# 52 groups of nine products behind the last real product of a two-block transformer kernel

## The reference, cut to what matters

```python
def sq_relu_mlp(h, w_in, w_out):
    return jnp.square(jax.nn.relu(h @ w_in)) @ w_out
...
    m_lat = sq_relu_mlp(modulate(rms_norm(x, g_mlp_pre[i]), sh2, sc2), w_mlp_in[i], w_mlp_out[i])
    x = x + gt2 * rms_norm(m_lat, g_mlp_post[i])
...
return x
```

## Time and profile before

| | |
|---|---|
| median of 2 runs | 3484.51 us |
| the runs | 3483.55 and 3485.47 us |
| span of the profiled execution | 3485.0 us |
| PE busy | 3435.7 us (99%), 18494 records |
| DVE, ACT, POOL busy | 2166.1 (62%), 1318.3 (38%), 297.0 us (9%) |
| mean granted clock of PE | 0.996 |
| DMA | 452.01 MB, mean 130 GB/s |

### The profile page before, as it was taken

One profiled execution on the slowest core, in us unless ns is written; L12 is line 12 of the kernel. 1 busy time (PEld: TensorE's weight loads), 2 busy tenths in 40 slices (PEclk: granted clock), 3 DMA queues, 4 the chain that ended last, 5 costly groups with the idle time before them and its releaser, 6 DMA issues.

```text
span 3485.0 us, 46915 instructions
## 1 busy us (share of the span) xinstructions
PE 3435.7 (99%) x18494; PEld 2869.0 (82%) x18494; DVE 2166.1 (62%) x3570; ACT 1318.3 (38%) x1951; POOL 297.0 (9%) x376
## 2 busy tenths in 40 slices
PE   9999999999999999999999999999999999999998
PEld 7888967898888988895789888899988898588888
DVE  7555565656555655566676777788776557655444
ACT  4222453333222422246333523355523236643222
POOL 0000232001000100023100000012100001210000
PEclk9999999999999999999999999999999999999999
DMA  7544302434444344330243444345444311013221
GB/s 277 187 157 160 109 24 100 157 133 169 155 160 150 137 165 156 146 108 10 102 163 138 148 160 157 145 147 180 173 171 163 112 70 67 25 50 119 89 95 49
DMA packets 85562, 452.01 MB, mean 130 GB/s; under 512 B 10305, under 2 KB 12545, under 8 KB 48609
## 3 DMA queue, kind: packets, MB, share of 16 engines
q1 hardware_dynamic: 83168, 439.10, 34.2%
q0 software_dynamic: 2176, 9.92, 0.8%
HBM read 446.88 MB, written 2.10 MB: 129 GB/s over the span
## 4 chain that ended last, share of the span: by engine, by line
PE 89%; DVE 5%; ACT 3%; issue 1%; DMA 0%; POOL 0%; DVEq 0%; SPq 0%; ACTq 0%; POOLq 0%
PE ps L660 22%; PE ps L658 22%; PE ps L659 22%; PE ps L2774 2%; PE ps L2775 2%; PE ps L2776 2%; PE ps L3473 1%; PE ps L1035 1%; PE ps L1037 1%; ACT P L1855 1%; PE ps L1036 1%; PE ps L1772 1%; PE ps L1295 1%; PE ps L1297 1%; PE ps L1296 1%
## 5 line engine op out<-in xcount | busy, mean ns | idle before, releaser
L660 PE MATMUL ps<-nH,WL 128*128 128x512 f32 x2256 | 884.9, 392 | 0.0
L658 PE MATMUL ps<-nH,WH 128*128 128x512 f32 x2256 | 884.3, 392 | 0.4 <-ACT rot L3203 0.4
L659 PE MATMUL ps<-nL,WH 128*128 128x512 f32 x2256 | 883.1, 391 | 0.0
L564 DVE TENSOR_TENSOR WL<-raw,WH 128x2048 fp32r<-128x2048 f32 (+2 forms) x297 | 651.0, 2196 | 372.3 <-ACT WH L553 371.2
L553 ACT ACTIVATE WH<-raw 128x2048 fp32r<-128x2048 f32 (+2 forms) x299 | 543.3, 1822 | 574.4 <-PE ps L660 496.9
L658 PEld LDWEIGHTS ps<-nH,WH 128*128 128x128 f32 x2256 | 423.8, 188 | 95.2 <-issue 3.3
L659 PEld LDWEIGHTS ps<-nL,WH 128*128 128x128 f32 x2256 | 423.8, 188 | 93.7 <-issue 0.2
L660 PEld LDWEIGHTS ps<-nH,WL 128*128 128x128 f32 x2256 | 423.8, 188 | 91.5
L624 DVE SCALAR_TENSOR_TENSOR araw<-araw,cB 128x1024 f32<-128x1024 f32 x224 | 275.4, 1229 | 208.2 <-DMA araw<-in_ast 207.9
L658 PE MATMUL ps<-hH,WH 128*128 128x512 f32 x944 | 372.2, 394 | 1.0 <-DVE h L1262 1.0
L660 PE MATMUL ps<-hH,WL 128*128 128x512 f32 x944 | 371.3, 393 | 0.0
(11 more groups left out here) (452 smaller groups left out, 5919.6 us busy)
## 6 DMA issues: line engine op xcount, KB each, us to landing
raw<-in_wst SPq DMA_DIRECT2D x273, 1024.0 KB, 4.8
araw<-in_ast SPq DMA_DIRECT2D x225, 512.0 KB, 5.7
raw<-in_wst SPq DMA_DIRECT2D x18, 512.0 KB, 3.3
araw<-in_wst SPq DMA_DIRECT2D x9, 1024.0 KB, 4.8
row<-in_ast SPq DMA_DIRECT2D x15, 512.0 KB, 10.5
cw<-in_cw POOLq DMA_DIRECT2D x4, 1024.0 KB, 6.0
h<-in_xT SPq DMA_DIRECT2D x4, 512.0 KB, 5.5
raw<-in_wst SPq DMA_DIRECT2D x8, 256.0 KB, 2.7
```

Source lines behind the costliest of these rows:

```text
L564: dve.q.tensor_tensor(M.WL[k % NW][:, 0:n], M.raw[raw_use[k]][:, 0:n], M.WH[k % NW][:, 0:n].bitcast(F32), ALU.subtract).then_inc(*v_wlo.up(k))
L658: pe.q.matmul(to, hi[:, i, cc], xh, start=i == 0, stop=False)
L659: pe.q.matmul(to, hi[:, i, cc], xl, start=False, stop=False)
L660: t = pe.q.matmul(to, lo[:, i, cc], xh, start=False, stop=i == nk - 1)
```

## The change

A function `end_pe` is added, and PE's program calls it last. It takes the next two banks, `aside` for products of `ones` and `to` for the groups. It issues 20 pairs of products of `ones`, then 52 groups with such a pair behind each, and one product of `ones` at the end, which counts up a semaphore that nobody waits for. A group is nine products: three blocks of weights of slot 0 with the three terms each. Their moving operand begins at column 512 (i // 3) plus a shift. 16 groups are 512 columns wide with shifts from 48 to 108 in steps of 4 columns (16 bytes); 32 are 256 wide with shifts from 16 to 140 in steps of 4; four are 512 wide with the shift 48, and begin 0, 16, 32 and 48 columns further in the weights. What `nH`, `nL` and the slot hold then is what the kernel left there. The results are read by nobody.

```diff
+        def end_pe(pe):
+
+            nh, nl = (x[:, :, :].rearrange("p a b -> p (a b)") for x in (lat.nH, lat.nL))
+            two = [take("end", x) for x in range(2)]
+            for b, free in two:
+                pe.wait_ge(*free)
+            to, aside = two[0][0], two[1][0]
+
+            def between():
+                for _ in range(2):
+                    pe.q.matmul(aside[:, 0:128], M.ones[:, :], M.ones[:, :], start=True, stop=True)
+
+            def group(N, n, shift, at=0):
+                for i in range(n):
+                    w, x = ((0, 0), (0, 1), (1, 0))[i % 3]
+                    c = 512 * (i // 3) + shift
+                    pe.q.matmul(to[:, 0:N], (M.WL[0] if w else M.WH[0])[:, 128 * (i // 3) + at:128 * (i // 3) + 128 + at],
+                                (nl if x else nh)[:, c:c + N], start=i == 0, stop=i == n - 1)
+                between()
+
+            for _ in range(20):
+                between()
+            for x in range(16):
+                group(512, 9, 48 + 4 * x)
+            for x in range(32):
+                group(256, 9, 16 + 4 * x)
+            for x in range(4):
+                group(512, 9, 48, 16 * x)
+            t = pe.q.matmul(aside[:, 0:128], M.ones[:, :], M.ones[:, :], start=True, stop=True)
+            t.then_inc(*mm.up("end", 1))
+
...
             rest_pe(pe, attention2_pe(pe))
+            end_pe(pe)
```

## The result

The changed kernel took 3592.79 us (3590.22 and 3595.36) against 3484.51 before: a ratio of 1.0305, with a 95% interval of 1.0284 to 1.0325. It is slower by 3%, as forecast; the time is 6.8 us above the forecast of 3586. It lies inside the range of 3579 to 3597, but above the 3582 to 3590 to which the forecast gave 0.80.

The account below looks back on a forecast made before the run. PE, 99% busy, bounds the kernel. Tail start 3476.8 us plus clock 1.5, ones 32.4, groups 41.6 and 34.0, last record 0.2 and meeting 0.2 gave span 3586.7; less 0.5, 3586 us, range 3579 to 3597.

Parts of the forecast that it names:

- What bounds the kernel, and the cover: PE, busy for 99% of the span, bounds the kernel; its work ends 8.1 us before the end, hiding that much tail.
- Steps, not durations: In the groups, a product costs the distance between starts; pricing by durations would add 151 us, twice too much.
- The price of the places: In the groups, 0.231 us per 512-wide and 0.118 per 256-wide product: 41.6 and 34.0 us, nothing for shifted weights.
- Products of ones: In the tail, 145 products of two records each at 0.1117 us a record: 32.4 us.
- The clock: The tail begins in a trough at half clock, costing 1.5 us (1.0 to 3.0), with no further fall expected.
- The start and the banks: The tail starts at 3476.8 us, behind the root's spread, without waiting for its two banks, freed earlier by VectorE.
- From the span to the time: At the sum's end, 0.5 us off the 3586.7 span, since the span before was 3485.0 and the median 3484.5.
- Dearer places: Rival in the groups: shifted places cost longer steps, 3622 us in all or 3595 for a quarter of groups; chance 0.10.
- Cheaper places: Rival in the groups: shifted places cost shorter steps, 70.9 us for the groups and 3581 in all; chance 0.07.
- Clock, bank and end: Tail rivals: clock stays at half, 3692; bank freed late, 3592; end isn't PE's, time stays 3484.5; chance 0.01 each.

Follow-up runs that it names:

- e2_cover: The changed kernel without all groups and all but 13 products of ones, against the kernel before: 3484.99 us against 3484.21, ratio 1.0002.
- e3_ones_only: The changed kernel without the groups, keeping the 145 products of ones: 3510.11 us, ratio 1.0075 to the kernel before.
- e5_one_place: The changed kernel with all shifts of the 52 groups set to 0: 3586.15 us against 3485.00 for the kernel before, ratio 1.0294.
- e1_again: The changed kernel once more, unchanged, beside the kernel before: 3587.94 us against 3484.21, ratio 1.0296.
- e4_groups_only: The changed kernel without the products of ones but the last, keeping the 52 groups: 3553.07 us, ratio 1.0199 to the kernel before.
- e11_gap16_both: The kernel before, no tail, with 16-column gaps ahead of the weight slots and the second block's hidden layer: 3468.00 us against 3485.19, ratio 0.9954.

## Why the prediction was right

**What bounds the kernel, and the cover.** Right. In e2_cover a tail of PE that fits costs nothing, and e3_ones_only shows 7.9 us of cover where the forecast had 8.1. The whole tail can't tell it so closely: 110 us of tail cost 101.2 in e5_one_place and 103.7 in e1_again.

**Steps, not durations.** Right, and the largest number in it: 75.8 us measured for the groups (75.9 in e4_groups_only) against 75.6; by durations it would have been 151.

**The price of the places.** Right in sum, by luck of the mean: 0.231 and 0.118 stood between the rows, and in e5_one_place the kernel's own places give the same groups to 0.4 us. A part of the reasoning was wrong. The forecast put the spread of its 256-wide rows, 0.114 to 0.120, down to where the operands lie; but the 0.114 and the 0.118 are of the same tiles in the same network, and are the two rhythms of one place. The bounds for single places were too narrow for the 512-wide ones. The forecast let 512 columns go from 0.229 to 0.236; long stretches show 0.2268 to 0.2397. "I add nothing for the shift" of the weights was wrong as a rule: 1 column there changes the step by 2%, 16 by 1%. For four groups of nine it doesn't show.

**Products of ones.** Right: 25.9 us for e3_ones_only against 26 expected.

**The clock.** Right: one trough, 1.5 us, then full clock.

**The start and the banks.** Right, no wait. The start itself was 3478.3 in the profiled run and 3476.66 in e1_again, against 3476.8.

**From the span to the time.** This is the part of the sum that was off by a few us. The sum took 0.5 us off the span to come to the median. In the runs after, the time stands 1.8 us above the span (3590.22 against 3588.4; 3587.94 against 3586.1 in e1_again). So the execution profiled before, with a span of 3485.0, was itself some 2.3 us above the median of its kernel; the two nearly cancel in the difference of 101.7, and what is left is scatter. The first measurement, of two runs, gave 108; e1_again gave 103.7 and e5_one_place 101.2. The profiled run of the first measurement carried the slow step of its first network, 7 us, and was spared three troughs of at most 1.7 us each. For the second run, 5.1 us above it, there is no trace. Its mean granted clock is 0.997 as in e1_again, so the troughs are back, and e1_again's 3587.9 with 7 us more would be 3594.9 where it measured 3595.4; that it carried the slow step too is likely and not shown. The forecast had no term for a part ahead of the tail that differs by 7 us from one execution to the next, and that is likely why the first measurement left the 3582 to 3590.

**The rivals.** Dearer places: single ones are, by 3% with a shift of 108 columns, which the change has, and by 5% with a shift of 1, which it hasn't; but not in the mean of these groups, and only the first product of a group, behind the ones, has the step of 0.31 to 0.32; the 512-wide ones behind it stay below 0.24. Cheaper places: they exist, 1% below the kernel's own, and too few to show. Clock, bank and end: out, by the windows, the timeline and e3_ones_only. The Trainium skill's page "TensorE: Matmul & The Clock Gate" gave 0.216 and 0.131 us for 512 columns (section "Back-to-back issue gap"); the shortest step of a long stretch in any run here is 0.227, so the trace agrees with neither.

## What to carry to other kernels

Price a matmul stream by the distance of its starts, never by the durations of its records, and read that distance at several tiles: where the moving operand and the weights lie to each other in SBUF is worth up to 5% of it. A short row of steps can mislead, since one place can have two rhythms: take a hundred steps or more, and from several executions. Here an unused tile of 64 bytes ahead of the weights took 13.5 us off a kernel that is 99% bound by PE. Try the gap for the width that holds most products, and look at the other widths before moving on.

Work behind an engine's last instruction is free up to the end of what the others still do, and costs its full length from there, though nobody reads it. Measure a kernel like this in several runs: one network's worth of steps came out 2% longer in two of fourteen executions with nothing changed in it.

## What the runs showed of the hardware that was not expected

- The step of a 512-wide float32r product at full clock depends on the places of both reads: 226.8 ns where they begin alike within 256 bytes (two stretches, and three tiles in the runs with gaps), up to 239.7 ns with the moving operand 4 bytes further than the kernel's own place. Shifting both by 4 bytes gives 236.2 instead of 228.9, so it isn't their distance alone.
- For 256 columns the same like beginning is bad: 0.1200 us in e11_gap16_both, against 0.1178 or 0.1133 with the hidden layer 64 bytes ahead of the weights.
- At one place a stream can have two rhythms and hold either over more than a hundred products: 0.1178 and 0.1133 us at 256 columns, 0.229 and 0.233 at 512. In the two changes shown here it changed behind a break or a longer first step.
- The 512-wide stream at shift 0 found 228.9 ns within some five products in all of 36 starts that were tried; yet the first network held 0.233 us instead of 0.229 for some 330 us in two executions of fourteen. What decides that is open.
